# The passage from the output projection into the feed-forward products, in another order

## The chip, the cores and the metric

The kernel runs on one core of one Trainium2 chip. The metric is the device time of one execution in microseconds (us), taken as the median of several runs.

## What is computed

Two layers of a hybrid encoder run over 576 tokens: 512 of a prompt and 64 of a sample (d_model 1024, feed-forward width 2816, all in float32). The part that matters here is the end of a layer, cut from the reference:

```python
merged = concat([rms_norm(o_att), rms_norm(o_gm)], -1)   # 1024 wide
x = x + merged @ p['w_o']
h2 = rms_norm(x, p['g_ffn'])
x = x + (silu(h2 @ p['w_gate']) * (h2 @ p['w_up'])) @ p['w_down']
```

## The kernel before

All activations lie transposed, features on the 128 partitions and 576 tokens along the row: `xT` holds x in 8 tiles of 128 features. Float32 products are made from split operands: a high part (`hs_hi`, `w_hi`, `t_hi`: a copy in the fp32r format) and a low part (`hs_lo`, `w_lo`, `t_lo`: the value less its high part); each product is three matmuls, hi x hi, hi x lo and lo x hi. ScalarE makes high parts, VectorE the low parts of activations, GpSimd the low parts of weights.

**The engines' order.** Nothing is scheduled by a tool. Each engine has its own program, written out by hand and run in order, with waits on semaphores between them. `Ring` and `Slots` count, while the program is planned, which value of `full` (TensorE's finished products) and of the other semaphores a reader has to wait for, and which PSUM bank is free.

**The output projection.** `w_o` is done in eight output tiles (`out_tile`), in the order `W_O_ORDER`: tiles 0, 4, 1, 5, 2, 6, 3, 7. A tile is 48 matmuls of 288 columns (8 tiles of features, 3 matmuls, 2 halves of the tokens). VectorE adds each tile to x (`add`, L1665), ScalarE squares it (`square`, L949) and GpSimd adds the squares up (`sum_squares`, L770) in `sumsq`.

**The feed-forward products.** Gate and up matrices are taken in blocks of 256 columns, and each block is multiplied by Strassen's scheme: 7 products of quarter size (12 matmuls each) instead of 8. Products P1 and P2 use parts of x (`hs_hi`, `hs_lo`), P6, P5, P4, P7 and P3 use sums. On the side of x these are four sums t1 to t4 of halves of x per pair of feature tiles (`x_sum(k)`, L1676 to L1684, k from 0 to 3; ScalarE scales an operand first in `x_scale`), split by ScalarE (`t_high`, L1175) and VectorE (`x_low`, L1690). On the side of the weights VectorE adds quarters (`sum_in`, `w_sum`, L1703), ScalarE copies (`high_in`) and GpSimd subtracts (`low_piece`, L861): five pieces per matrix, two of them without a sum. `sum_in(j, up_in, gate_in, 1)` for j from 0 to 3 are the sums of the first up block, `sum_in(j, n0, up_in, 2)` those of the loop's first gate block. `L["g0"]` is the first gate block, `L["u0"]` the first up block; the other ten pairs of blocks, with the down projection, run in a loop.

**The passage.** `first_block` is written for the stretch in which x is not finished. TensorE begins with the parts of P6, P5 and P4 for k = 0, 1, 2 (27 matmuls), then P1 (its parts k need `hs_lo` of tiles 0 to 3, columns 0 to 287), then the last quarters of P6, P5, P4 (k = 3), P7, the squares' sum by token (`sums_by_token`, L1945, ten tiny matmuls), P2 (tiles 4 to 7) and P3. ScalarE copies P1 out (`first_product`, L1204). VectorE's `evict` forms u2 (L1728, from P6) and u3 (L1731, from P7), and c22, c21, c11, c12 from the rest; P7 waits for u2, P3 for c22. `evict` calls a function handed over in `between` after a named step.

**The root.** The normalization factor is 1/sqrt of the mean square: `r_asked` reads the token sums out of PSUM, GpSimd takes the root (`root`, L761), `r_taken` copies it (L1364), TensorE spreads it over the columns (`r_along_columns`, L2259) and VectorE copies it to `rb` and multiplies the gate block by it (L1821), before its own loop preparations and the up block's `evict`.

VectorE's program in the passage, as it stands before (L1797 on):

```python
add(3)
for j in range(4):
    sum_in(j, up_in, gate_in, 1)
add(7)
x_sum(3)
for k in range(4):
    low_part(2 * l + 1, k, g_ffn, half)
x_low(3)
low_part(2 * l + 1, 4, g_ffn)
```

GpSimd waits for the last `x_low` before it adds squares 6 and 7 (L883).

## Time and profile before

| | |
|---|---|
| median of 3 runs | 1406.43 us |
| lowest and highest | 1401.91 and 1406.65 us |
| the profiled execution | 1408.31 us |
| its span in the profile | 1406.5 us |
| TensorE busy | 1349.6 us, 96% of the span |
| VectorE, ScalarE, GpSimd busy | 912.5, 600.2, 855.4 us |
| mean granted TensorE clock | 0.983 of full speed |

In the profile L numbers are lines of the kernel, PE is TensorE's matmuls, PEld its weight loads, DVE VectorE, ACT ScalarE, POOL GpSimd. A matmul of 288 columns is listed with some 0.29 us, but the next one starts 0.13 us after it: starts tell the pace. Behind "<-" in brackets stands what ended the idle time. All times in a timeline are from the start of the span.

### The profile page before, as it was taken

The page shows a single profiled execution, that of the slowest core. Times are in us where ns is not written, and L with a number is a line of the kernel's source. Part 1 is how long each engine was busy: PE and PEld are TensorE (multiplying, and loading weights), DVE is VectorE, ACT ScalarE, POOL GpSimd, SP SyncE. Part 2 cuts the span into 40 slices and gives each one's busy share as a digit, 9 for nine tenths or more (in the row PEclk, how much of TensorE's full clock was granted, in tenths as well). Part 3 has the DMA queues.
Part 4 walks back from the last instruction along what each step waited for, and adds up shares of the span by engine and source line. Part 5 has one row for each costly group of instructions (what it writes and reads, how often), then busy time and mean ns, then how long its engine had stood idle before and what let it go on. Part 6 is the DMA issues. An engine that isn't in the chain of part 4 may idle for free.

```text
span 1406.5 us, 25387 instructions
## 1 busy us (share of the span) xinstructions
PE 1349.6 (96%) x9462; PEld 1245.9 (89%) x9462; DVE 912.5 (65%) x1490; ACT 600.2 (43%) x956; POOL 855.4 (61%) x452
## 2 busy tenths in 40 slices
PE   8999989989999999999999989989899999999998
PEld 7885667989999999999988656779899999999997
DVE  3456567586676767676736465756876666666664
ACT  6237476353333333333432455763433333333331
POOL 2445247377777777777654534455687777777771
PEclk9999999999999999999999999999999999999999
DMA  7200022122333222222412000221122223223221
GB/s 231 83 16 15 1 60 61 31 61 85 92 91 92 89 90 90 90 89 89 130 61 68 11 5 1 61 61 54 41 87 91 89 90 90 91 89 91 91 85 68
DMA packets 138593, 102.35 MB, mean 73 GB/s; under 512 B 8988, under 2 KB 125152, under 8 KB 138528
## 3 DMA queue, kind: packets, MB, share of 16 engines
q1 hardware_dynamic: 135864, 100.46, 23.6%
q10 hardware_dynamic: 2664, 1.02, 0.3%
q8 instruction: 42, 0.69, 0.2%
q14 instruction: 23, 0.19, 0.0%
HBM read 98.10 MB, written 3.36 MB: 72 GB/s over the span
## 4 chain that ended last, share of the span: by engine, by line
PE 84%; DVE 8%; ACT 2%; issue 2%; POOL 2%; DMA 1%; ACTq 0%; SPq 0%; DVEq 0%
PE ps L2234 34%; PE ps L1932 9%; PE ps L1933 9%; PE ps L1936 9%; PE ps L1878 4%; PE ps L1915 3%; PE ps L1917 3%; PE ps L1916 3%; PE ps L2175 2%; PE ps L2155 2%; POOL rs L761 2%; PE ps L2039 2%; PE ps L2045 1%; PE ps L2132 1%; DVE hs_lo L1330 1%
## 5 line engine op out<-in xcount | busy, mean ns | idle before, releaser
L761 POOL TENSOR_TENSOR rs<-ms,mhalf 128x8 f32<-128x8 f32 (+5 forms) x66 | 139.7, 2120 | 196.8 <-DVE ms L1468 78.9
L861 POOL TENSOR_TENSOR w_lo<-raw,w_hi 128x1024 fp32r<-128x1024 f32 x132 | 229.8, 1768 | 42.4 <-ACT w_hi L1281 39.7
L1703 DVE TENSOR_REDUCE raw<-raw 128x512 f32<-128x1024 f32 x184 | 230.5, 1254 | 0.5
L861 POOL TENSOR_TENSOR w_lo_a<-raw,w_hi_a 128x512 fp32r<-128x512 f32 x88 | 179.6, 2053 | 69.9 <-ACT w_hi_a L1281 69.9
L1932 PE MATMUL ps<-act_hi,w_hi 128*128 128x288 f32 x704 | 196.6, 294 | 3.5 <-issue 3.5
L1933 PE MATMUL ps<-act_lo,w_hi 128*128 128x288 f32 x704 | 196.9, 295 | 0.0
L1665 DVE TENSOR_TENSOR xT<-ps,xT 128x576 f32<-128x576 f32 x192 | 142.2, 750 | 46.9 <-PE ps L1936 46.8
L2234 PE MATMUL ps<-t_hi,w_hi 128*128 128x288 f32 x528 | 157.8, 299 | 7.4 <-DVE side L1728 6.2
L2234 PE MATMUL ps<-t_lo,w_hi 128*128 128x288 f32 x528 | 157.3, 298 | 0.0
L2234 PE MATMUL ps<-t_hi,w_lo 128*128 128x288 f32 x528 | 157.0, 297 | 0.0
L754 POOL TENSOR_TENSOR w_lo<-raw,w_hi 128x2048 fp32r<-128x2048 f32 (+1 forms) x21 | 93.4, 4452 | 97.8 <-ACT w_hi L929 97.8
L1936 PE MATMUL ps<-act_hi,w_lo 128*128 128x288 f32 x704 | 150.9, 296 | 0.0
L1281 ACT ACTIVATE w_hi<-raw 128x512 fp32r<-128x512 f32 (+1 forms) x120 | 88.8, 770 | 121.7 <-DVE raw L1703 121.7
L1932 PEld LDWEIGHTS ps<-act_hi,w_hi 128*128 128x128 f32 x704 | 132.9, 189 | 3.9 <-issue 3.9
L1933 PEld LDWEIGHTS ps<-act_lo,w_hi 128*128 128x128 f32 x704 | 133.0, 189 | 0.0
L909 POOL TENSOR_TENSOR w_lo<-raw,w_hi 128x2048 fp32r<-128x2048 f32 x20 | 92.5, 4625 | 66.4 <-ACT w_hi L1295 66.4
L1936 PEld LDWEIGHTS ps<-act_hi,w_lo 128*128 128x128 f32 x704 | 113.3, 189 | 0.0
L2234 PEld LDWEIGHTS ps<-t_hi,w_hi 128*128 128x128 f32 x528 | 99.9, 189 | 8.7 <-issue 7.0
L2234 PE MATMUL ps<-hs_hi,w_hi_a 128*128 128x288 f32 x352 | 104.0, 296 | 3.7 <-DVE hs_lo L1330 3.7
L2234 PE MATMUL ps<-hs_hi,w_lo_a 128*128 128x288 f32 x352 | 103.5, 294 | 0.0
L2234 PE MATMUL ps<-hs_lo,w_hi_a 128*128 128x288 f32 x352 | 103.3, 293 | 0.0
L2234 PEld LDWEIGHTS ps<-t_hi,w_lo 128*128 128x128 f32 x528 | 100.8, 191 | 0.0
(245 smaller groups left out, 3473.1 us busy)
## 6 DMA issues: line engine op xcount, KB each, us to landing
raw<-in_w_gate SPq DMA_DIRECT2D x88, 256.0 KB, 3.7
raw<-in_w_up SPq DMA_DIRECT2D x88, 256.0 KB, 3.6
raw<-in_w_down SPq DMA_DIRECT2D x20, 1024.0 KB, 4.9
raw<-in_w_in SPq DMA_DIRECT2D x9, 1024.0 KB, 5.2
raw<-in_w_o SPq DMA_DIRECT2D x16, 512.0 KB, 5.5
x_tm<-in_x_prompt SPq DMA_DIRECT2D x4, 512.0 KB, 4.9
raw<-in_w_down SPq DMA_DIRECT2D x8, 256.0 KB, 3.5
out_y_prompt<-x_tm SPq DMA_DIRECT2D x8, 256.0 KB, 2.2
```

Of the source, the lines that this page charges most:

```text
L754: pool.tensor_tensor(w_lo[:, k % 2, 0:size], raw[:, n % 2, 0:size], w_hi[:, k % 2, 0:size].bitcast(F32), ALU.subtract).then_inc(lo_split, 1)
L761: pool.tensor_tensor(rs[:, c:c + n], ms[:, c:c + n], mhalf[:, 0:n], ALU.pow).then_inc(rs_ready, 1)
L861: pool.tensor_tensor(lo[:, k, cols], src, hi[:, k, cols].bitcast(F32), ALU.subtract).then_inc(lo_split, 1)
L909: pool.tensor_tensor(w_lo[:, k % 2, :], raw[:, n % 2, :], w_hi[:, k % 2, :].bitcast(F32), ALU.subtract).then_inc(lo_split, 1)
L1281: act.activation(hi[:, k, cols], src, ACT.Copy).then_inc(hi_split, 1)
L1665: return dve.tensor_tensor(x, ps[:, u.bank:u.bank + 2, 0:HALF], x, ALU.add)
L1703: dve.tensor_reduce(raw[:, 2, j * Q:(j + 1) * Q], added(a, b), AX.X, ALU.add).then_inc(sums_added, 1)
L1878: return pe.transpose(dst, src, ident[0:n, 0:n])
L1932: pe.matmul(bank(u, cols=HALF), hi, x_hi[:, k, cols], start=first, stop=False)
L1933: pe.matmul(bank(u, cols=HALF), hi, x_lo[:, k, cols], start=False, stop=False)
L1936: ins = pe.matmul(bank(u, cols=HALF), lo, x_hi[:, k, cols], start=False, stop=last)
L2234: ins = pe.matmul(bank(u, cols=HALF), a_w[:, k_w, w], x_k(k), start=start, stop=False, skip_group_check=True)
```

## The change

- The last output tile takes its feature tiles in the order 0 to 7, and TensorE signals when its first half is done (`wo_half`). ScalarE makes the high parts of tiles 0 to 3 (which write over what that half has read) after that signal, and those of tiles 4, 5, 6 directly after the whole tile.
- On VectorE the low parts of tiles 0 to 3 come before the last addition to x; two of the four weight sums of the first up block come behind the whole `evict` of the gate block.
- The last split of sums (k = 3) is cut in two halves on ScalarE and VectorE, with a count of their own; TensorE's last quarters wait for the half they use.
- Low part 7 comes behind u3. GpSimd adds squares 6 and 7 only when all low parts are made. Odd squares go to `hid[:, 1]` instead of `gate[:, 1]`.
- The squares' sum by token stands behind P3 on TensorE instead of before P2, and the spreading of the root behind P6 of the up block instead of behind P1.

```diff
-        L["wo"] = {m: [ring.add("wo_added", with_last=h > 0) for h in range(2)] for m in W_O_ORDER}
+        L["wo"] = {}
+        for no, m in enumerate(W_O_ORDER):
+            if no == KT - 1:
+                L["wo_half"] = ring.mark()
+            L["wo"][m] = [ring.add("wo_added", with_last=h > 0) for h in range(2)]
...
-        L["g0"] = block(L["ffn_in"][0], FIRST_PRODUCTS, {"P7": sums})
+        L["g0"] = block(L["ffn_in"][0], FIRST_PRODUCTS, {"P3": sums})
...
-        L["u0"] = block(L["ffn_in"][1], between={"P1": columns})
+        L["u0"] = block(L["ffn_in"][1], between={"P6": columns})
...
+        def squares_of(m, no):
+
+            if m % 2 == 0 and no % 2:
+                return hid[:, 1, :]
+            return gate[:, no % 2, :]
...
-                pool.wait_ge(t_lo_done, KT // 2 * (l + 1))
+                pool.wait_ge(hs_lo_done, (2 * l + 2) * KT)
                 sum_squares(2 * l, [6, 7])
                 low_piece(up_in, 2)
                 root(l, "r2", NT)
...
-                filled(act, L["wo"][W_O_ORDER[-1]][1])
+                filled(act, L["wo_half"])
                 for k in range(4):
                     high_part(k, g_ffn, half)
-                t_high(3)
+                filled(act, L["wo"][W_O_ORDER[-1]][1])
+                for k in range(4, 7):
+                    high_part(k, g_ffn)
+                t_high(3, 0, 2)
+                t_high(3, 2, 4)
+                first_product(L["g0"], L["g0"].out["u2"] - 1)
                 square_output(7)
-                high_part(4, g_ffn)
+                high_part(7, g_ffn)
                 high_in(up_in, 2, slots.last[L["w_o"][3]], SUMS * l + 4)
-                high_part(5, g_ffn)
-                high_part(6, g_ffn)
-                first_product(L["g0"], L["g0"].out["u2"] - 1)
-                high_part(7, g_ffn)
...
-                for j in range(4):
+                for j in range(2):
                     sum_in(j, up_in, gate_in, 1)
+                for k in range(4):
+                    low_part(2 * l + 1, k, g_ffn, half)
                 add(7)
                 x_sum(3)
-                for k in range(4):
-                    low_part(2 * l + 1, k, g_ffn, half)
-                x_low(3)
+                x_low(3, 0, 2)
+                x_low(3, 2, 4, 1)
                 low_part(2 * l + 1, 4, g_ffn)
...
-                def more_low_parts():
-                    for k in range(5, KT):
+                def low_parts(first, last):
+                    for k in range(first, last):
                         low_part(2 * l + 1, k, g_ffn)
-                    dve.wait_ge(summed, (2 * l + 1) * KT)
 
                 evict(L["g0"], first_p1 + 1, gate, None, (0, 0, 0), None,
-                      {"u2": more_low_parts, "c22": lambda: r_asked(L["ss2"]),
-                       "c11": lambda: r_taken(l, "r2", 2 * l + 2)})
+                      {"u2": lambda: low_parts(5, 7), "u3": lambda: low_parts(7, KT),
+                       "c21": lambda: dve.wait_ge(summed, (2 * l + 1) * KT - 1)})
+                r_asked(L["ss2"])
+                for j in range(2, 4):
+                    sum_in(j, up_in, gate_in, 1)
+                r_taken(l, "r2", 2 * l + 2)
...
-                    out_tile(no)
+                    if no < KT - 1:
+                        out_tile(no)
+                        continue
+                    out_tile(no, range(KT // 2)).then_inc(full, 1)
+                    out_tile(no, range(KT // 2, KT))
...
                     made("u2")
                     product(b.b, w_sum(2), k_w, x_sum(2), False)
-                    pe.wait_ge(summed, (2 * l + 1) * KT)
-                    sums_by_token(L["ss2"], [sumsq])
                     pe.wait_ge(p1_out, copied)
                     product(b.a, a_part(1), k_w, x_part(1, 0), False, ready=lambda k: part_due(k + KT // 2))
                     pe.wait_ge(lo_split, split + 5)
                     made("c22")
                     product(b.c, w_sum(3), k_w, x_part(1, 1), False)
+                    pe.wait_ge(summed, (2 * l + 1) * KT)
+                    sums_by_token(L["ss2"], [sumsq])
...
                     product(b.a, a_part(0), k_w, x_part(0, 0), True)
-                    between()
                     pe.wait_ge(lo_split, split + 3)
                     free_in_turn(b.b)
                     product(b.b, w_sum(1), k_w, x_sum(1), True)
+                    between()
```

VectorE at the start of the passage, from the split of the sums k = 2 on, before the change (`xT<-ps,xT` is an addition to x, `raw<-raw` a weight sum, `hs_lo` a low part, `side` u2):

```order
L1690 TENSOR_TENSOR t_lo<-x_sums,t_hi 128x4x288
L1665 TENSOR_TENSOR xT<-ps,xT 128x576
L1703 TENSOR_REDUCE raw<-raw 128x512 x4
L1665 TENSOR_TENSOR xT<-ps,xT 128x576
L1676 SCALAR_TENSOR_TENSOR x_sums<-xT,gT,x_sums 128x288
L1679 SCALAR_TENSOR_TENSOR x_sums<-xT,gT,x_sums 128x288
L1682 SCALAR_TENSOR_TENSOR x_sums<-xT,gT,x_sums 128x288
L1684 SCALAR_TENSOR_TENSOR x_sums<-xT,gT,x_sums 128x288
L1330 SCALAR_TENSOR_TENSOR hs_lo<-xT,gT,hs_hi 128x288 x4
L1690 TENSOR_TENSOR t_lo<-x_sums,t_hi 128x4x288
L1330 SCALAR_TENSOR_TENSOR hs_lo<-xT,gT,hs_hi 128x576
L1728 TENSOR_TENSOR side<-ps,side 128x288
```

The same place after the change:

```order
L1702 TENSOR_TENSOR t_lo<-x_sums,t_hi 128x4x288
L1677 TENSOR_TENSOR xT<-ps,xT 128x576
L1715 TENSOR_REDUCE raw<-raw 128x512 x2
L1342 SCALAR_TENSOR_TENSOR hs_lo<-xT,gT,hs_hi 128x288 x4
L1677 TENSOR_TENSOR xT<-ps,xT 128x576
L1688 SCALAR_TENSOR_TENSOR x_sums<-xT,gT,x_sums 128x288
L1691 SCALAR_TENSOR_TENSOR x_sums<-xT,gT,x_sums 128x288
L1694 SCALAR_TENSOR_TENSOR x_sums<-xT,gT,x_sums 128x288
L1696 SCALAR_TENSOR_TENSOR x_sums<-xT,gT,x_sums 128x288
L1702 TENSOR_TENSOR t_lo<-x_sums,t_hi 128x2x288 x2
L1342 SCALAR_TENSOR_TENSOR hs_lo<-xT,gT,hs_hi 128x576
L1740 TENSOR_TENSOR side<-ps,side 128x288
```

The four low parts now stand ahead of the addition of tile 7 and of the sums of x; two weight sums have left.

VectorE from u3 of the gate block to u2 of the up block, before the change (`ms` and `r_tok` belong to the root, `rb` to the spread factor):

```order
L1731 TENSOR_TENSOR side<-ps,side 128x288
L1734 TENSOR_TENSOR gate<-side,ps 128x288
L1356 TENSOR_SCALAR ms<-ps 128x5
L1359 COPY ms<-ms 128x5
L1737 TENSOR_TENSOR gate<-side,ps 128x288
L1746 COPY gate<-ps 128x288
L1364 COPY r_tok<-rs 128x5
L1749 TENSOR_TENSOR gate<-ps,side 128x288
L1816 COPY rb<-ps 128x512
L1818 COPY rb<-ps 128x64
L1821 TENSOR_TENSOR gate<-gate,rb 128x576 x2
L1703 TENSOR_REDUCE raw<-raw 128x512 x2
```

The same place after the change, without the first two rows' like (u3 and low part 7 stand ahead of it):

```order
L1747 TENSOR_TENSOR gate<-side,ps 128x288
L1750 TENSOR_TENSOR gate<-side,ps 128x288
L1759 COPY gate<-ps 128x288
L1762 TENSOR_TENSOR gate<-ps,side 128x288
L1368 TENSOR_SCALAR ms<-ps 128x5
L1371 COPY ms<-ms 128x5
L1715 TENSOR_REDUCE raw<-raw 128x512 x2
L1376 COPY r_tok<-rs 128x5
L1833 COPY rb<-ps 128x512
L1835 COPY rb<-ps 128x64
L1838 TENSOR_TENSOR gate<-gate,rb 128x576 x2
L1715 TENSOR_REDUCE raw<-raw 128x512 x2
```

The root is asked for behind the whole `evict`, and the two weight sums stand between the question and the copy of its answer.

## Rows read from the trace of the kernel before

**Rows 1.** The page: busy us by engine, and the chain by engine.
```profile
PE 1349.6 (96%) x9462; PEld 1245.9 (89%) x9462; DVE 912.5 (65%) x1490; ACT 600.2 (43%) x956; POOL 855.4 (61%) x452
...
PE 84%; DVE 8%; ACT 2%; issue 2%; POOL 2%; DMA 1%; ACTq 0%; SPq 0%; DVEq 0%
```

**Rows 2.** Stretches: length, busy us (instructions) of each engine, PEclk, DMA share, GB/s.
```profile
304.04:338.39 34.35, 28.80 (x190) 27.74 (x189) 27.99 (x39) 16.03 (x24) 23.79 (x15) 0.90 0.20 61
996.94:1031.30 34.36, 28.82 (x191) 27.76 (x189) 28.00 (x39) 16.03 (x24) 23.81 (x15) 0.90 0.20 60
400.00:600.00 200.00, 200.00 (x1512) 200.00 (x1511) 136.42 (x194) 73.30 (x99) 149.63 (x75) 1.00 0.30 90
```

**Rows 3.** Timeline of TensorE in the first passage: start, us, line, operation [idle before].
```profile
309.62 0.37 PE L2234 MATMUL ps<-hs_hi,w_hi_a 128*128 128x288 f32 x1 [1.84 <-DVE hs_lo L1330]
...
312.09 0.40 PE L2234 MATMUL ps<-t_hi,w_hi 128*128 128x288 f32 x1 [0.61 <-DVE t_lo L1690]
...
314.70 0.50 PE L2234 MATMUL ps<-t_hi,w_hi 128*128 128x288 f32 x1 [1.15 <-DVE side L1728]
...
317.64 1.44 PE L1945 MATMUL ps<-ones,sumsq 128*128 128x1 f32 x10
...
330.43 0.37 PE L2234 MATMUL ps<-t_hi,w_hi 128*128 128x288 f32 x1 [1.93 <-DVE side L1728]
```

**Rows 4.** Stretches of one microsecond, columns as in rows 2.
```profile
316.00:317.00 1.00, 1.00 (x6) 1.00 (x6) 1.00 (x2) 0.00 (x0) 1.00 (x1) 0.50 0.00 0
333.00:334.00 1.00, 1.00 (x6) 1.00 (x6) 0.98 (x2) 0.00 (x0) 1.00 (x2) 0.50 0.00 0
```

**Rows 5.** Timeline of ScalarE: the last scaling and the four high parts.
```profile
301.05 0.52 ACT L1187 ACTIVATE x_sums<-xT,gT 128x288 f32<-128x288 f32 x1
304.24 1.82 ACT L943 ACTIVATE hs_hi<-xT,gT 128x288 fp32r<-128x288 f32 x4 [2.67 <-PE ps L1936]
```

**Rows 6.** Timeline of GpSimd: squares' sums, weight pieces, the root.
```profile
302.12 1.46 POOL L770 TENSOR_TENSOR sumsq<-sumsq,gate 128x576 f32<-128x576 f32 x1
303.50 1.33 POOL L861 TENSOR_TENSOR w_lo_a<-raw,w_hi_a 128x512 fp32r<-128x512 f32 x1
304.77 2.42 POOL L861 TENSOR_TENSOR w_lo_a<-raw,w_hi_a 128x1024 fp32r<-128x1024 f32 x1
...
312.11 3.49 POOL L770 TENSOR_TENSOR sumsq<-sumsq,gate 128x576 f32<-128x576 f32 x2 [4.92 <-DVE t_lo L1690]
...
315.56 2.88 POOL L861 TENSOR_TENSOR w_lo<-raw,w_hi 128x1024 fp32r<-128x1024 f32 x1
...
320.99 1.18 POOL L761 TENSOR_TENSOR rs<-ms,mhalf 128x5 f32<-128x5 f32 x1 [2.56 <-DVE ms L1359]
...
333.93 2.38 POOL L861 TENSOR_TENSOR w_lo<-raw,w_hi 128x1024 fp32r<-128x1024 f32 x1
```

**Rows 7.** Timeline of VectorE in the first passage.
```profile
305.42 0.73 DVE L1665 TENSOR_TENSOR xT<-ps,xT 128x576 f32<-128x576 f32 x1
306.19 1.31 DVE L1676 SCALAR_TENSOR_TENSOR x_sums<-xT,gT,x_sums 128x288 f32<-128x288 f32 x1
...
308.96 1.80 DVE L1330 SCALAR_TENSOR_TENSOR hs_lo<-xT,gT,hs_hi 128x288 fp32r<-128x288 f32 x4
...
310.68 1.35 DVE L1690 TENSOR_TENSOR t_lo<-x_sums,t_hi 128x1152 fp32r<-128x1152 f32 x1
...
314.47 1.75 DVE L1330 SCALAR_TENSOR_TENSOR hs_lo<-xT,gT,hs_hi 128x576 fp32r<-128x576 f32 x1
...
316.14 3.64 DVE L1330 SCALAR_TENSOR_TENSOR hs_lo<-xT,gT,hs_hi 128x576 fp32r<-128x576 f32 x2
...
322.20 1.25 DVE L1364 COPY r_tok<-rs 128x5 f32<-128x5 f32 x1 [0.45 <-POOL rs L761]
...
327.39 2.53 DVE L1703 TENSOR_REDUCE raw<-raw 128x512 f32<-128x1024 f32 x2
...
329.83 0.45 DVE L1728 TENSOR_TENSOR side<-ps,side 128x288 f32<-128x288 f32 x1
```

More of the change, by code:

```diff
@@ L241 @@
 WARM = 24
+T_PARTS = KT // 2 + 1
 SMALL, EARLY_GAINS, LATE_GAINS = 8, 3, 8
@@ L1170, in _, with t_high @@
                     act.activation(hs_hi[:, k, 0:SEQ], bank(u), ACT.Copy, scale=gT[:, g:g + 1]).then_inc(m_hi, 1)
-                def t_high(k):
-                    act.wait_ge(x_summed, 4 * (KT // 2 * l + k + 1))
-                    act.activation(t_hi[:, :, k, :], x_sums[:, k % 2, :, :], ACT.Copy).then_inc(t_hi_done, 1)
+                def t_high(k, c0=0, c1=4):
+                    act.wait_ge(x_summed, 4 * (KT // 2 * l + k) + c1)
+                    act.activation(t_hi[:, c0:c1, k, :], x_sums[:, k % 2, c0:c1, :], ACT.Copy).then_inc(t_hi_done, 1)
                 def square_output(no):
@@ L1184, in x_scale @@
                     if k >= 2:
-                        act.wait_ge(t_lo_done, KT // 2 * l + k - 1)
+                        act.wait_ge(t_lo_done, T_PARTS * l + k - 1)
                     g = G_FFN + KT * l + k
@@ L1685, in x_sum, with x_low @@
                                              ).then_inc(x_summed, 1)
-                def x_low(k):
-                    dve.wait_ge(t_hi_done, KT // 2 * l + k + 1)
-                    dve.tensor_tensor(t_lo[:, :, k, :], x_sums[:, k % 2, :, :], t_hi[:, :, k, :].bitcast(F32), ALU.subtract
-                                      ).then_inc(t_lo_done, 1)
+                def x_low(k, c0=0, c1=4, part=0):
+                    dve.wait_ge(t_hi_done, T_PARTS * l + k + part + 1)
+                    dve.tensor_tensor(t_lo[:, c0:c1, k, :], x_sums[:, k % 2, c0:c1, :], t_hi[:, c0:c1, k, :].bitcast(F32),
+                                      ALU.subtract).then_inc(t_lo_done, 1)
                 def w_sum(j, n, landed, lower, base):
@@ L1731, in evict @@
                     dve.tensor_tensor(u3, p_b, p1, ALU.subtract).then_inc(S["ffn_out"], 1)
+                    follow("u3")
                     made("u3")
@@ L1938, in by_feature @@
                             ins.then_inc(full, 1)
+                return ins
             def sums_by_token(u, tiles):
@@ L2181, in out_tile @@
                 def out_tile(no, ks=None):
-                    by_feature(L["wo"][W_O_ORDER[no]], slots.raw[L["w_o"][no // 2]] % 2, no % 2 * P, COLS, KT, hs_hi, hs_lo,
-                               order=MERGED[1:], ks=ks, ready=None if no else lambda k: emptied(pe, L["mt"][k]))
+                    order = MERGED[1:] if no < KT - 1 else list(range(KT))
+                    return by_feature(L["wo"][W_O_ORDER[no]], slots.raw[L["w_o"][no // 2]] % 2, no % 2 * P, COLS, KT, hs_hi, hs_lo,
+                                      order=order, ks=ks, ready=None if no else lambda k: emptied(pe, L["mt"][k]))
                 pe.wait_ge(gm_normed, NT * (l + 1))
@@ L2268, in made, with sums_due @@
                         pe.wait_ge(S["ffn_out"], b.out[name])
-                    def sums_due(k):
-                        pe.wait_ge(t_lo_done, KT // 2 * l + k + 1)
+                    def sums_due(k, part=0):
+                        pe.wait_ge(t_lo_done, T_PARTS * l + k + part + 1)
                     def part_due(k):
@@ L2282, in first_block @@
                     product(b.a, a_part(0), k_w, x_part(0, 0), True, ready=part_due)
-                    sums_due(3)
-                    for u, w, x in early:
+                    for (u, w, x), part in zip(early, (0, 0, 1)):
+                        sums_due(3, part)
                         product(u, w, k_w, x, False, range(3, 4))
```

4 lines of the change are left out of this document (2 added, 2 removed).

## The prediction

> **What bounds the kernel now.** I read the page's busy row and its chain first. TensorE is busy for 96% of the span and has 84% of the chain that ended last [rows 1], so a change that adds no matmul pays only where TensorE stands still. The table of stretches tells where that is [rows 2]. Between 400 and 600 us, inside the feed-forward loop, 1512 matmuls fill 200.00 us: 0.132 us each, at full clock, without a gap. In the passage, from the first matmul on sums of x at 304.04 to the first of the loop at 338.39, 168 products' matmuls should take 168 x 0.132 = 22.2 us and the stretch has 34.35 us. The second layer's passage has 34.36 us. So the passage loses 12.1 us per layer, 24 us in all, 1.7% of the kernel; nothing else is touched.
>
> The timeline of TensorE in that stretch shows the loss [rows 3]: four gaps, of 1.84, 0.61, 1.15 and 1.93 us by the rows. The first ends when the low parts of x are there, the second with the low parts of the sums, the other two with u2 of the first and of the second block. A chain of ten tiny matmuls (the squares' sum by token, 1.3 us to the next product) stands between P7 and P2 of the first block, and ten more between two products of the second. The rest is clock: the windows at 316 and 333 us hold 6 matmuls per us, granted 0.50 (1.2 GHz), against 7.6 at full clock [rows 4]; each time some 12 matmuls cost 0.24 instead of 0.13 us, 1.3 us.
>
> **Where VectorE and GpSimd meet.** They hold each other up. Four low parts of 288 columns take 1.80 us, 0.45 each, at 308.96 when GpSimd stands idle; one of 576 columns takes 1.75 us at 314.47, ending 0.6 us after GpSimd's sums (312.11 for 3.49) have ended at 315.60; the next two take 3.64 us at 316.14, while GpSimd's split (315.56 for 2.88) ends at 318.44 [rows 6, 7]. The split in turn took 2.88 instead of 2.42 us: it waited for the low part. The weight sums (tensor_reduce, one operand) and the additions out of PSUM are not held up. So: an instruction of VectorE with two operands in SBUF starts when GpSimd's running instruction has ended, and GpSimd's next one waits for it; they alternate.
>
> The Trainium skill, page SBUF — State Buffer, in its section on the two separate sides, speaks against this change: VectorE's instructions with two SBUF inputs and GpSimd's share one exclusive lock, held for a whole instruction. By bare durations the low parts would be 1.8 us of work wherever they are put, and the sum would come out near the first rival below; by the lock it comes out as below. The rows above show the lock.
>
> **The change, step by step** (times as in the trace of before; first layer).
>
> 1. *The half signal.* The last output tile's 48 matmuls end at 304.04, so its first half ends 24 x 0.132 = 3.2 us sooner, 300.9. ScalarE is busy to about 301.5 with the scaling at 301.05, then makes the four high parts at 301.5 to 303.3 instead of 304.24 to 306.06 [rows 5]: 2.7 us sooner.
>
> 2. *VectorE.* The addition of tile 3 and two weight sums end at 302.9 (two sums take 2.53 [rows 7]). Now the four low parts are due, before the last addition. GpSimd runs its sum from 302.12 to 303.58, a piece of 512 (303.50, some 1.3) and one of 1024 (2.42) [rows 6]. Alternating: low part 0 ends at 303.9, GpSimd's 512 at 305.2, low part 1 at 305.6, GpSimd's 1024 at 308.0, low parts 2 and 3 at 308.8. What would be 1.8 us takes 5.9. The addition of tile 7 follows, 308.8 instead of 305.42. The two other weight sums (2.5 us) have left, so the four steps of the sums of x run free, each about 0.53: 309.5 to 311.6 against 306.19 to 309.0 before (the low parts start at 308.96). The cut in halves saves 0.5 us: the first half's low part is ready at 311.9, the second at 312.7, against 312.03 for the whole [rows 7].
>
> 3. *TensorE, first block.* P1 starts right behind the early ones, 307.6 instead of 309.62; its last quarter waits for low part 3 and ends at 309.2. Then the gap moves: 2.7 us until 311.9. u2 comes behind low part 4 and is ready at about 313.9, and P7 starts at 314.1 instead of 314.70: gain 0.6. The squares' chain is gone from here; low parts 5 and 6 run free, GpSimd waiting. Low part 7 now waits for u3, so for P7's end (about 316.2): ready at 317.4. P2 ends at 317.9, P3 at 319.5, where before the chain of ten sat at 317.64 and P3 ended at 322.4: 2.9 us gained so far.
>
> 4. *The squares' sum comes later.* GpSimd adds the last two squares only after low part 7: 317.4 to 320.2 (1.4 each; before they began at 312.11). TensorE waits 0.9 us, runs its ten, and P1 of the second block starts at 321.5: 0.9 of the 2.9 us is left. GpSimd then has the third up piece (2.4) before the root (1.18): the root ends at 323.8, where before it ended at 322.17 [rows 6]. VectorE is at the two delayed weight sums from 322.0 to 324.6, and its copy of the roots, which needs the lock (1.25 us for 5 columns at 322.20 [rows 7]), waits for GpSimd's next piece: done at 325.3 instead of 323.45, 1.85 late. The spreading over columns on TensorE, which stood 6.4 us ahead of u2 together with the two rb copies, two multiplications and two more weight sums (323.45 to 329.83 [rows 7]), is 5.9 us now, since c12 has gone ahead: u2 at 331.2, 1.4 late. P6 of the up block no longer waits behind the spreading, but its P7 waits for u2: gap from 328.0 to 331.8, where it was 328.3 to 330.43.
>
> 5. *The squares in another buffer, the counter T_PARTS, two instructions more on VectorE and ScalarE:* nothing, since ScalarE stands idle from 306 to 309 and the added halves are in step 2. The load of w_down waits for the last up piece and is issued some 2 us later than now; its weights are used 10 us after it landed, so it hides there.
>
> Sum: the loop begins 1.4 us later per layer, if both half-clock stretches stay as they are. Two layers: +2.8 us. The profiled execution took 1408.31 us (span 1406.5), so 1411.1; it stands 1.9 above the median of the three runs, 1406.43, and against that median the forecast is **1409.2 us**. Bounds per layer: the alternation costs 4.1 us in step 2 at most and nothing at least; the half-clock stretches may become none (-2.6) or three (+1.3).
>
> **Rivals.**
> - *The low parts slip through* (the other side). If GpSimd's pieces do not hold the low parts, they end at 304.8 and the addition of tile 7 at 305.5; the first step of the sums of x still waits for GpSimd until 307.2, as now, the halves are ready at 309.1 and 309.9, P7 starts at 311.3, 2.8 us sooner than in my sum, and all behind it follows: the loop begins 1.4 us sooner than before, 2.8 us in all, 1403.6. For: only low parts of 576 columns were seen held. Against: the first step of the sums, also 288 columns, took 1.31 us at 306.19 and ended 0.3 us after GpSimd's 1024 piece [rows 6, 7]. The sign turns once the low parts lose less than 2.7 us to GpSimd instead of 4.1. Chance 0.2.
> - *The clock goes another way.* Gaps of 2.7 and 3.8 us replace smaller ones, four in number as before; which matmuls run at 1.2 GHz depends on where the idle lies. One stretch fewer in each layer: 2.6 us off, 1406.6. Chance 0.15. One more in each, or the slow stretch falling on a full product: 2.6 to 4 us on, 1412 to 1413. Chance 0.12.
> - *The tail starves the loop.* GpSimd's first pieces for the loop end 1.4 to 2 us later. The third now ends at 336.3 (333.93 for 2.38 [rows 6]) and is wanted by the loop's second product, 12 x 0.132 = 1.6 us after 338.39, at 340.0, so 1.5 us or more remain. If they do not, each layer loses another 2 us: 1413. Chance 0.05.
>
> The forecast itself has 0.48.
>
> **How the numbers follow.** About 0.5%, 7 us, is what a measurement of this kernel can tell from no change. Faster than 1399.4 needs the first rival and a lost clock stretch: 0.12. Slower than 1413.5 needs the forecast and an added stretch in both layers, or a mis-sized step 4: 0.16. The rest, 0.72, is within. The range takes in the first rival, less one lost clock stretch (1403.6 - 2.6 = 1401.0), and the slower clock at 1413.5.
>
> **What would show it.** Right: in the profile after, P1 of the first block starts at once behind the early products; the low parts of 288 columns spread over some 5 us between GpSimd's pieces; a gap of over 2 us sits in front of the last quarter of the early products; the gap in front of the second block's u2 is over 3 us. Wrong: four low parts within 2 us, a passage shorter than 33 us, or u2 of the second block ahead of 25.8 us after the passage's start.

## The result, and the profile after

| | before | after |
|---|---|---|
| median of 12 runs each | 1407.84 us | 1413.3 us |
| lowest and highest | 1401.91, 1411.86 | 1409.52, 1418.38 |
| the profiled execution | 1408.31 | 1413.44 |
| its span | 1406.5 | 1411.6 |
| mean granted TensorE clock | 0.983 | 0.981 |

The ratio is 1.0039, with a 95% interval of 1.0023 to 1.0056: the kernel is 5.5 us slower. That is 0.4%, less than the 0.5% that the prediction took as what a measurement can tell, but the interval is clear of 1. The forecast was 2.8 us slower, 1409.2 us, in a range to 1413.5.

The stretches of the trace after, with the columns of [rows 2]: the two passages, the last four products of the first passage, and a piece of the loop.

```profile
307.36:344.89 37.53, 30.15 (x190) 29.04 (x189) 28.06 (x39) 14.63 (x21) 24.15 (x15) 0.86 0.18 56
1000.05:1037.86 37.81, 29.89 (x190) 28.76 (x189) 28.06 (x39) 14.63 (x21) 24.14 (x15) 0.86 0.18 55
335.67:344.89 9.22, 9.22 (x48) 9.22 (x49) 5.10 (x7) 2.60 (x4) 8.89 (x5) 0.66 0.01 3
403.00:603.00 200.00, 200.00 (x1512) 200.00 (x1511) 136.40 (x194) 74.06 (x99) 147.09 (x74) 1.00 0.31 94
```

The loop is what it was, 1512 matmuls in 200 us. The passages are 3.2 and 3.5 us longer than the 34.35 and 34.36 us of [rows 2], 6.6 us together. This profiled execution is only 5.1 us longer than that of before, since the rest of it comes out 1.5 us shorter. No instruction was changed there, but half-clock stretches outside the passages fall at other places (the granted clock is 0.50 from 823.4 to 830.2 us before, and from 133.7 to 140.5 us after); that these make up the 1.5 us was not worked out.

The timeline of TensorE after, first passage; the gaps answer to [rows 3].

```profile
315.16 0.40 PE L2257 MATMUL ps<-t_hi,w_hi 128*128 128x288 f32 x1 [2.49 <-DVE t_lo L1702]
...
317.19 0.37 PE L2257 MATMUL ps<-t_hi,w_hi 128*128 128x288 f32 x1 [0.53 <-DVE side L1740]
...
323.36 0.83 PE L1963 MATMUL ps<-ones,sumsq 128*128 128x1 f32 x6 [0.78 <-POOL sumsq L781]
...
335.66 0.58 PE L2257 MATMUL ps<-t_hi,w_hi 128*128 128x288 f32 x1 [3.49 <-DVE side L1740]
336.04 0.45 PE L2257 MATMUL ps<-t_lo,w_hi 128*128 128x288 f32 x1
336.28 0.45 PE L2257 MATMUL ps<-t_hi,w_lo 128*128 128x288 f32 x1
```

The 1.84 us gap ahead of P1 is gone. In its place stand 2.49 us ahead of the last early quarters, and in front of the second block's P7 3.49 us instead of 1.93. Behind that gap the starts are 0.24 us apart, at half clock. In the second layer the gap ahead of u2 of the first block is gone, one of 1.07 us stands ahead of the spreading of the root, and P7 has 3.50 us in front of it.

VectorE after, from the low parts on, answering to [rows 7]:

```profile
306.14 5.54 DVE L1342 SCALAR_TENSOR_TENSOR hs_lo<-xT,gT,hs_hi 128x288 fp32r<-128x288 f32 x4
311.60 0.75 DVE L1677 TENSOR_TENSOR xT<-ps,xT 128x576 f32<-128x576 f32 x1
312.38 0.52 DVE L1688 SCALAR_TENSOR_TENSOR x_sums<-xT,gT,x_sums 128x288 f32<-128x288 f32 x1
...
325.56 2.59 DVE L1715 TENSOR_REDUCE raw<-raw 128x512 f32<-128x1024 f32 x2
328.06 0.85 DVE L1376 COPY r_tok<-rs 128x5 f32<-128x5 f32 x1
330.45 0.69 DVE L1833 COPY rb<-ps 128x512 f32<-128x512 f32 x1 [1.54 <-PE ps L2282]
...
331.31 1.43 DVE L1838 TENSOR_TENSOR gate<-gate,rb 128x576 f32<-128x576 f32 x2
332.66 2.50 DVE L1715 TENSOR_REDUCE raw<-raw 128x512 f32<-128x1024 f32 x2
335.08 0.44 DVE L1740 TENSOR_TENSOR side<-ps,side 128x288 f32<-128x288 f32 x1
```

Four low parts of 288 columns took 1.80 us in [rows 7]; here they take 5.54. The last row is u2 of the second block, 27.7 us after the passage's start (335.08 - 307.36), where it was 25.8 (329.83 - 304.04). GpSimd shows why the root is late: the last two squares begin at 320.33, 13.0 us into the passage, where in [rows 6] they began at 312.11, 8.1 us in.

```profile
305.46 1.42 POOL L781 TENSOR_TENSOR sumsq<-sumsq,hid 128x576 f32<-128x576 f32 x1
306.85 4.08 POOL L872 TENSOR_TENSOR w_lo_a<-raw,w_hi_a 128x512 fp32r<-128x512 f32 x2
320.33 1.42 POOL L781 TENSOR_TENSOR sumsq<-sumsq,gate 128x576 f32<-128x576 f32 x1 [9.39 <-DVE hs_lo L1342]
321.89 1.42 POOL L781 TENSOR_TENSOR sumsq<-sumsq,hid 128x576 f32<-128x576 f32 x1
323.26 2.35 POOL L872 TENSOR_TENSOR w_lo<-raw,w_hi 128x1024 fp32r<-128x1024 f32 x1
325.73 1.18 POOL L772 TENSOR_TENSOR rs<-ms,mhalf 128x5 f32<-128x5 f32 x1
```

### The profile page after: what moved, and what is told of

It is laid out like the page before. It is cut to its first block, busy times and chain, and to the rows that moved or that the text cites. A ratio compares the mean times of both kernels' runs of the same rounds, so it can differ in the third digit from the quotient of the medians.

```text
span 1411.6 us, 25389 instructions
## 1 busy us (share of the span) xinstructions
PE 1350.9 (96%) x9462; PEld 1247.5 (88%) x9462; DVE 913.9 (65%) x1492; ACT 600.5 (43%) x958; POOL 853.4 (60%) x452
## 4 chain that ended last, share of the span: by engine, by line
PE 84%; DVE 9%; ACT 2%; POOL 2%; issue 2%; DMA 1%; ACTq 0%; SPq 0%; DVEq 0%; POOLq 0%
PE ps L2257 34%; PE ps L1949 9%; PE ps L1953 9%; PE ps L1950 9%; PE ps L1895 4%; PE ps L1932 3%; PE ps L1933 3%; PE ps L1934 3%; PE ps L2193 2%; PE ps L2173 2%; DVE hs_lo L1342 2%; POOL rs L772 2%; PE ps L2057 2%; PE ps L2063 1%; PE ps L2150 1%
```

## The experiments

In all of them times are given from the start of the passage (the first matmul on sums of x), and "P7" alone is that of the second block. "Half clock costs" is what the matmuls that start while the granted clock is 0.50 lose against 0.132 us each, summed over the passage (worked out from the starts in the timelines). Executions of one kernel lie 6 to 17 us apart, with the granted clock over the whole of them, so where there is a single one the passage in its trace is the measurement, and not the time. Each ratio is to executions of the kernel before on the same chip; their medians were 1407.23 to 1409.14 us, and 1404.36 us for the last row.

| kernel | P7 of block 1 | P7 | loop begins | half clock costs | gap ahead of P7 | ratio to before |
|---|---|---|---|---|---|---|
| before, layers 1 / 2 | 10.7 / 10.7 | 26.4 / 26.4 | 34.4 / 34.4 | 2.5 / 2.5 | 1.9 | 1 |
| after | 9.8 / 10.2 | 28.3 / 28.7 | 37.5 / 37.8 | 4.1 / 3.7 | 3.5 | 1.0039 [1.0023, 1.0056] |
| low parts back | 9.4 / 9.3 | 27.8 / 27.8 | 35.8 / 35.8 | 2.9 / 2.8 | 3.5 | one execution |
| GpSimd waits | 9.6 / 8.6 | 28.7 / 27.1 | 36.5 / 35.0 | 4.0 / 2.8 | 3.5 | one execution |
| spreading back | 10.1 / 9.3 | 28.6 / 27.6 | 35.0 / 34.0 | 1.1 / 1.0 | 1.9 | one execution |
| sums back | 10.6 / 10.3 | 29.4 / 29.0 | 38.3 / 37.9 | 4.8 / 3.7 | 3.5 | one execution |
| squares back | 9.3 / 10.2 | 27.8 / 28.3 | 36.8 / 36.1 | 3.4 / 2.3 | 3.6 | one execution |
| front alone | 9.7 / 10.6 | 26.5 / 27.1 | 34.5 / 35.0 | 2.6 / 3.5 | 1.9 | 0.9989 [0.9961, 1.0016] |
| tail alone | 10.7 / 10.6 | 30.1 / 30.5 | 38.1 / 38.5 | 3.0 / 4.1 | 3.5 | 1.0063 [1.0038, 1.0087] |
| after, P4 ahead | 10.1 / 9.3 | 28.6 / 27.8 | 33.5 / 32.7 | 1.2 / 1.5 | 1.9 | 1.0001 [0.9971, 1.0031] |
| after, u2 first | 9.3 / 10.5 | 25.1 / 26.6 | 31.6 / 33.0 | none / 1.1 | 1.1 | 1.0 [0.997, 1.003] |
| before, u2 first | 10.7 / 10.7 | 24.3 / 24.3 | 30.7 / 30.7 | 1.1 / 1.1 | none | 0.9967 [0.9943, 0.999] |
| front, u2 first | 10.3 / 9.7 | 25.1 / 24.4 | 31.4 / 30.8 | 1.0 / 1.1 | none | 0.9979 [0.9958, 0.9999] |
| before, P4 ahead | 10.6 / 10.7 | 26.4 / 26.4 | 31.3 / 31.3 | none / 1.1 | 0.4 | 1.0003 [0.9976, 1.0031] |

### Is it the low parts, and does GpSimd hold them?

Two kernels on the changed one. First the low parts at their old place:

```diff
-                for k in range(4):
-                    low_part(2 * l + 1, k, g_ffn, half)
                 add(7)
                 x_sum(3)
+                for k in range(4):
+                    low_part(2 * l + 1, k, g_ffn, half)
```

> The changed kernel with one part undone: on VectorE the addition of tile 7 and the sums of x stand ahead of the four low parts again. All numbers from the passage's first matmul on sums of x. Lock theory (low parts of 288 columns wait for GpSimd's pieces): the four low parts take 1.8 us in one go instead of 5.4, the last quarter of the early products starts at 7.6 instead of 7.8, P7 at 9.5 instead of 9.8, and the loop begins within 0.4 us of the changed kernel's 37.5, because the tail (root, two late weight sums, u2 behind two loop sums) is as it was. Rival (the low parts' place is what made the kernel slower): the loop begins at 35 or sooner, the time falls by 5 us or more.

Second, the low parts ahead as in the change, but GpSimd's pieces wait for them:

```diff
                 sum_squares(2 * l, [5])
+                pool.wait_ge(hs_lo_done, (2 * l + 1) * KT + 4)
                 low_piece(up_in, 0)
```

> The changed kernel with one wait added: GpSimd starts the first two pieces of the up matrix only when low parts 0 to 3 are made. Lock theory: the four low parts take 1.8 us in one go at the place where the change puts them, and the addition of tile 7 moves from 4.2 us to about 1.1 us after the passage's start; the sums of x then meet GpSimd's two pieces and lose most of it again, P7 starts at 9.3 instead of 9.8 and the loop begins 0.3 to 0.5 us sooner. Rival (GpSimd doesn't hold VectorE up, the low parts wait for something else, such as ScalarE's high parts): the low parts keep their spread over 5 us and nothing moves.

VectorE in the first (an addition, two steps of the sums of x, then the low parts):

```profile
311.55 0.53 DVE L1688 SCALAR_TENSOR_TENSOR x_sums<-xT,gT,x_sums 128x288 f32<-128x288 f32 x1
312.11 2.54 DVE L1691 SCALAR_TENSOR_TENSOR x_sums<-xT,gT,x_sums 128x288 f32<-128x288 f32 x1
...
315.55 1.80 DVE L1342 SCALAR_TENSOR_TENSOR hs_lo<-xT,gT,hs_hi 128x288 fp32r<-128x288 f32 x4
```

and in the second:

```profile
303.98 2.36 DVE L1343 SCALAR_TENSOR_TENSOR hs_lo<-xT,gT,hs_hi 128x288 fp32r<-128x288 f32 x4
306.26 0.75 DVE L1678 TENSOR_TENSOR xT<-ps,xT 128x576 f32<-128x576 f32 x1
307.04 0.99 DVE L1689 SCALAR_TENSOR_TENSOR x_sums<-xT,gT,x_sums 128x288 f32<-128x288 f32 x1
308.06 2.54 DVE L1692 SCALAR_TENSOR_TENSOR x_sums<-xT,gT,x_sums 128x288 f32<-128x288 f32 x1
```

The same low parts take 5.54, 1.80 and 2.36 us, by what GpSimd runs beside them: its two pieces, nothing, and the end of its addition of squares (303.30 to 304.73), which holds the first low part until 305.05. What is next in VectorE's queue then meets the pieces instead: one step of 0.52 us takes 2.54, the length of GpSimd's piece of 1024. So the mutual holding up is real, and in each of these three orders some of it was paid while GpSimd's two pieces lay in these 4 us. Moving it is worth 0.5 to 0.8 us at block 1's P7 with the low parts back, 0.2 and 1.5 us with GpSimd waiting (at 9.6 and 8.6, where 9.3 was expected). The gap of 3.5 us ahead of the second block's P7 stays in both, and P7 stands 18.5 us behind P7 of block 1 in both layers with the low parts back, as after the change (15.7 before): so the loss of P7 lies behind block 1. The loop, however, begins at 35.8 with the low parts back, which neither expectation had (37.1 to 37.9, or 35 and sooner), and at 36.5 and 35.0 with GpSimd waiting, where some 37 was expected. The clock is most of that: from P7 to the loop TensorE takes 8.0 us with the low parts back and 7.8 and 7.9 with GpSimd waiting, instead of 9.2. The times were 1414.95 and 1413.14 us, not shorter than after the change.

### Front alone, tail alone

The front is the half signal, ScalarE's order, the low parts and the halves; the tail is the squares' sum with low part 7 behind u3, the spreading and the two weight sums. The front alone undoes these lines of the change:

```diff
-        L["g0"] = block(L["ffn_in"][0], FIRST_PRODUCTS, {"P3": sums})
+        L["g0"] = block(L["ffn_in"][0], FIRST_PRODUCTS, {"P7": sums})
-        L["u0"] = block(L["ffn_in"][1], between={"P6": columns})
+        L["u0"] = block(L["ffn_in"][1], between={"P1": columns})
-                pool.wait_ge(hs_lo_done, (2 * l + 2) * KT)
+                pool.wait_ge(t_lo_done, T_PARTS * (l + 1))
                 sum_squares(2 * l, [6, 7])
-                for j in range(2):
+                for j in range(4):
                     sum_in(j, up_in, gate_in, 1)
```

with VectorE's `between` functions and TensorE's two calls as they were; the tail alone makes just these, reversed, in the kernel before, with the squares' other buffer.

> The front of the change alone: half signal, ScalarE's new order, low parts ahead of the last addition, halves of the last split; the squares' sum, the spreading of the roots and all four weight sums at their old places. Theory A (the tail made the kernel slower, the front is worth next to nothing): the passage from first matmul on sums of x to the loop is 34 to 35 us (before 34.35, changed 37.5 and 37.8), P7 of the second block at 26.4 +-0.5, the time within 1.5 us of before (ratio 1.000 +-0.001). Rival B (the spread low parts of the front carry a part of the loss): the passage stays at 36 us or more, ratio 1.002 or more.

> The tail of the change alone, on the kernel before: the squares' sum behind the first block's last product and in another buffer, the spreading of the roots behind P6, two weight sums behind the first block; no half signal, old order of the low parts, the last split whole. Theory A (the tail carries the loss): P7 of the first block at 10.0 to 10.7, P1 of the second at 17.5 to 18.2, P7 of the second at 28 to 28.8 (before 26.4), the loop at 36.5 to 38 (before 34.35), some +2 to +3.5 us per layer, ratio 1.003 to 1.005. Rival B (the loss comes from the front, or from front and tail together): the loop at 35.5 or sooner, ratio under 1.002.

```profile
302.38:336.83 34.45, 28.88 (x190) 27.80 (x189) 29.33 (x39) 14.53 (x21) 23.59 (x15) 0.90 0.18 56
990.79:1025.83 35.04, 29.90 (x190) 28.91 (x189) 29.91 (x40) 14.53 (x21) 24.18 (x15) 0.85 0.19 59
```

are the two passages of the front alone, and

```profile
303.36:341.45 38.09, 29.18 (x191) 27.86 (x189) 27.37 (x39) 16.14 (x24) 22.80 (x15) 0.91 0.18 55
999.91:1038.36 38.45, 30.60 (x190) 29.32 (x189) 27.33 (x39) 16.14 (x24) 22.79 (x15) 0.87 0.17 54
```

those of the tail alone. The tail costs 3.7 and 4.1 us per layer and more time than the whole change (1.0063); the front costs 0.1 and 0.7 us in the trace and nothing in the time. Joined with the tail the front gives back 0.6 us per layer. The first theory holds: the tail is what made the kernel slower. It was expected to bring P7 to 28 to 28.8, the loop to 36.5 to 38 and the ratio to 1.003 to 1.005; all three came out beyond (30.1 and 30.5, 38.1 and 38.5, 1.0063). And its loss lies in the lateness of P7 alone. From P7 to the loop, in these rows of the stretches, the kernel before and the tail alone take the same time, although the gap in front is 1.93 us in the one and 3.50 in the other:

```profile
330.43:338.39 7.96, 7.96 (x48) 7.96 (x49) 5.04 (x7) 2.62 (x4) 7.96 (x5) 0.79 0.00 1
333.48:341.45 7.97, 7.97 (x49) 7.97 (x49) 5.04 (x7) 2.60 (x4) 7.97 (x5) 0.79 0.01 3
```

Why the front gains nothing in the end can be read too: it brings P7 of block 1 forward by 0.9 and 0.1 us, but GpSimd begins squares 6 and 7 0.5 and 1.0 us later (8.6 and 9.1 us into the passage, 8.1 before), and the roots are copied at 19.5 and 20.1 instead of 19.4.

### Which part of the tail?

Each undone by itself in the changed kernel. The spreading behind P1 again:

```diff
-        L["u0"] = block(L["ffn_in"][1], between={"P6": columns})
+        L["u0"] = block(L["ffn_in"][1], between={"P1": columns})
...
                     product(b.a, a_part(0), k_w, x_part(0, 0), True)
+                    between()
...
                     product(b.b, w_sum(1), k_w, x_sum(1), True)
-                    between()
```

> The changed kernel with one thing undone: in the second block TensorE spreads the roots over the columns right behind P1, as before, and no longer behind P6. Theory A (u2 of the second block is late because VectorE's queue ahead of it starts late, and about 1 us of that is TensorE finishing P6 before it spreads): the first copy of rb starts about 22.1 us after the start of the passage instead of 23.1, u2 comes 1 us sooner, the second block's P7 starts at 27.3 instead of 28.3 and the loop at 36.5 instead of 37.5; the gap ahead of P7 shrinks from 3.5 to some 1.5 us and a new one of 2.5 to 3 us stands ahead of P6. Rival B (the place of the spreading is hidden behind the late roots): P7 stays at 28.3, the loop at 37.5. Either way 2 us of the whole at most, so the passage in the trace decides.

The two weight sums ahead again (`range(2)` to `range(4)`, the later loop gone):

> The changed kernel with one thing undone: the two weight sums of the up weights that came later stand again right behind the first two, ahead of the four low parts. Theory A (they are not what makes u2 late, since VectorE does them while it waits for the root anyway): the low parts come up to 2.5 us later but run in fewer turns with GpSimd, P7 of the first block starts at 10.4 instead of 9.8, the copy of the roots ends at 21.0 to 21.5 (now 21.55), P7 of the second block starts at 27.7 to 28.3, the loop at 37 to 37.5. Rival B (the two sums in front of the copy of the roots hold it up by their 2.5 us): the copy ends by 19.5 to 20, P7 at 26.3, the loop at 35.5.

The squares' sum early again, its matmuls between P7 and P2, `r_asked` behind c22 and `r_taken` behind c11, low part 7 with the others behind u2:

```diff
-                pool.wait_ge(hs_lo_done, (2 * l + 2) * KT)
+                pool.wait_ge(t_lo_done, T_PARTS * (l + 1))
...
-                r_asked(L["ss2"])
                 for j in range(2, 4):
                     sum_in(j, up_in, gate_in, 1)
-                r_taken(l, "r2", 2 * l + 2)
```

> The changed kernel with one thing undone: the squares' sum and its ten matmuls at their old place between P7 and P2 of the first block, VectorE asking and taking the roots as before; the spreading stays behind P6, the two weight sums stay behind the first block. Theory A (the late squares' sum is the largest single part of the tail's loss): the copy of the roots ends at 18 to 19.5 us instead of 21.55, u2 of the second block at 25.8 to 27, its P7 at 26.5 to 27.7 and the loop at 34.5 to 35.7, the gap ahead of P7 below 3 us. Rival B (the roots come sooner but u2 stays behind VectorE's queue of sums, copies and products): P7 at 28 or later, the loop at 37 or more.

No single part brings P7 back to 26.4: it stands at 28.6 and 27.6, 29.4 and 29.0, 27.8 and 28.3. In time they were 1405.72, 1413.57 and 1413.93. With the squares back VectorE shows how one lateness hides another:

```profile
324.90 0.17 DVE L1376 COPY r_tok<-rs 128x5 f32<-128x5 f32 x1 [0.44 <-POOL rs L772]
...
325.91 2.63 DVE L1715 TENSOR_REDUCE raw<-raw 128x512 f32<-128x1024 f32 x2
329.42 0.69 DVE L1832 COPY rb<-ps 128x512 f32<-128x512 f32 x1 [0.88 <-PE ps L2281]
```

The roots are copied at 325.07, 18.0 us into the passage (start 307.09) and 3.6 us sooner than after the change (21.55). But now the two late weight sums and the spreading behind P6 stand between them and u2, and rb is copied at 22.3 instead of 23.1, only 0.8 us sooner. P7 (27.8 and 28.3) came out between the two expectations in the first layer and as the second had it in the other, the loop (36.8 and 36.1) between them. With the sums back the low parts start later, P1 of the second block starts at 19.1 and 18.8 instead of 17.1 and 17.7, and the squares that all wait for come later (ten matmuls at 18.0 and 17.6 instead of 16.0 and 16.6); the roots are copied at 22.8 and 22.5, and both expectations had the roots and P7 too early. With the spreading back P7 does not move by itself either: it stands at 28.6 and 27.6, but 18.5 and 18.3 us behind P7 of block 1, against 18.5 after the change. That is as the second theory said, yet the loop begins at 35.0 and 34.0, sooner than either had it. TensorE there:

```profile
328.03 1.38 PE L2282 MATMUL ps<-ident,r_tok 128*128 128x128 f32 x10 [2.63 <-DVE r_tok L1376]
...
334.53 0.37 PE L2257 MATMUL ps<-t_hi,w_hi 128*128 128x288 f32 x1 [1.93 <-DVE side L1740]
```

The idle time is cut in two pieces, 2.63 and 1.93 us, in place of one of 3.49 (in the second layer 1.49 and 1.93). The four products behind it run at full clock, in this row of the stretches:

```profile
334.52:340.98 6.46, 6.45 (x48) 6.46 (x49) 5.54 (x6) 1.94 (x3) 6.46 (x4) 1.00 0.00 1
```

6.46 us instead of 9.22 for the same 48 matmuls: 2.8 and 2.7 us in the two layers from the clock alone.

### The gap itself: P4 ahead of P7

P4 needs no u2. On TensorE alone, in the changed kernel:

```diff
+                    free_in_turn(b.d)
+                    product(b.d, a_part(2), k_w, x_sum(3), True)
                     pe.wait_ge(lo_split, split + 4)
                     made("u2")
                     product(b.b, w_sum(2), k_w, x_sum(2), False)
-                    free_in_turn(b.d)
-                    product(b.d, a_part(2), k_w, x_sum(3), True)
```

(for the first up block alone, with `FIRST_PRODUCTS` as the order in its plan).

> The changed kernel with one move on TensorE: in the second block P4, which needs no u2, ahead of P7. It changes nothing on VectorE, so u2 stays at 27.7 us after the passage's start and P7 at 28.3; the gap ahead of P7 is 1.9 instead of 3.5 us. Theory A (the gap of 3.5 us as one piece is what brings the half-clock stretch of 6.8 us behind it, some 2.8 us per layer): the loop begins at 33 to 34.5 us (now 37.5 and 37.8), 4 us sooner per layer, ratio to before 0.997 to 1.000. Rival B (the clock falls behind P7 anyway, whatever the gap's length): only the 1.6 us of P4 are won, the loop at 35.9 to 36.2, ratio 1.001 to 1.003.

```profile
300.96:334.44 33.48, 27.14 (x190) 26.00 (x189) 26.94 (x38) 13.95 (x20) 20.13 (x13) 0.95 0.20 62
991.07:1023.74 32.67, 27.39 (x190) 26.27 (x189) 26.40 (x38) 13.96 (x20) 19.63 (x13) 0.95 0.19 60
```

u2 is as late as it was (28.1 and 27.2), P7 starts at 28.6 and 27.8, and the loop begins 4.1 and 5.1 us sooner. The filled gap is 1.6 us of that. The 36 matmuls from P7 to the loop take 4.84 us, at full clock, where P7, P4, P2 and P3 took 9.22:

```profile
329.60:334.44 4.84, 4.84 (x36) 4.84 (x37) 3.94 (x6) 1.92 (x3) 4.84 (x3) 1.00 0.01 2
```

That is 2.8 us from the clock in each layer, what the first theory had; what is left, -0.3 and +0.8 us, is P7 itself, which comes with P7 of block 1. A new gap of 1.11 us opens in the loop's first block, outside the passage. The ratio is 1.0001 instead of 1.0039. It goes the same way, but its interval reaches to 1.0031 and just overlaps that of the change, so by the time alone the second theory (1.001 to 1.003) is not ruled out; the passages rule it out.

The same move in the kernel before:

> The kernel before with one move on TensorE: P4 of the second block ahead of P7, which fills its gap of 1.93 us but for 0.3. Theory A (a gap filled is worth its length, and the half-clock stretch behind it goes too, as in the same move on the changed kernel): P7 of the second block still at 26.4, behind P4, so that the loop begins at 31.4 to 32.7 us instead of 34.35, ratio 0.995 to 0.998. Rival B (the clock falls at the same place for what lies ahead of it): the loop at 32.7 or later, ratio 0.998 or more. The move of u2 on VectorE gave 30.7 us and 0.9967 for the same gap.

The passage is 31.26 and 31.27 us, 3.1 less than before, and here too a new gap of 1.11 us opens behind it in the loop:

```profile
339.40 0.40 PE L2234 MATMUL ps<-t_hi,w_hi 128*128 128x288 f32 x1 [1.11 <-DVE side L1728]
```

That leaves 2.0 us per layer, 4 in all, and a ratio of 0.997 was to be expected. The measured one is 1.0003, with an interval of 0.9976 to 1.0031. The profiled execution took 1400.2 us, others up to 1416.6. So the gain is seen in the one execution that has a trace and not in the median, and whether this move pays stays open.

### u2 first

VectorE does two weight sums for the loop ahead of u2 of the second block, 2.5 us for something that is wanted later. In the changed kernel and in the one before:

```diff
-                for j in range(2):
-                    sum_in(j, n0, up_in, 2)
+                def loop_sums():
+                    for j in range(3):
+                        sum_in(j, n0, up_in, 2)
...
-                      {"u2": lambda: sum_in(2, n0, up_in, 2), "c22": lambda: sum_in(3, n0, up_in, 2), "c21": gate_due})
+                      {"u2": loop_sums, "c22": lambda: sum_in(3, n0, up_in, 2), "c21": gate_due})
```

> The changed kernel with u2 of the up block made ahead of the loop's first two weight sums on VectorE (they follow directly behind it). Queue theory (u2 is late only because of what stands ahead of it on VectorE): P7 of the up block starts 2.5 us sooner, at 25.8 instead of 28.3 us of the passage, the gap in front of it shrinks from 3.5 to about 1 us, with it a stretch of half clock may vanish, and the loop begins 2.5 to 4 us sooner: 5 to 8 us less in all, 1405 to 1408. Rival (GpSimd's piece for P7 or the late root sets it): P7 gains less than 1 us, and the time stays within 2 us of the changed kernel's.

> The kernel before with the same one move as e3_u2_first. Queue theory: P7 of the up block starts 1.9 to 2.4 us sooner, the gap of 1.93 us in front of it closes, the half-clock stretch behind it goes with it (1.3 us), and the loop begins 2 to 3.7 us sooner: 1401 to 1404 against 1407.8, faster by 0.3 to 0.5%. Rival: the pieces of the loop's first block, now made 0.5 us later, hold up the loop's first products, and the time stays the same.

VectorE of the kernel before with this move, to be set beside the last rows of [rows 7]:

```profile
324.82 1.43 DVE L1821 TENSOR_TENSOR gate<-gate,rb 128x576 f32<-128x576 f32 x2
326.17 0.45 DVE L1728 TENSOR_TENSOR side<-ps,side 128x288 f32<-128x288 f32 x1
326.53 3.73 DVE L1703 TENSOR_REDUCE raw<-raw 128x512 f32<-128x1024 f32 x3
```

and its passages and the two new gaps of TensorE in the loop's first block:

```profile
302.79:333.50 30.71, 27.08 (x191) 26.23 (x189) 27.20 (x39) 15.37 (x24) 20.13 (x13) 0.94 0.22 68
995.54:1026.19 30.65, 27.09 (x190) 26.23 (x189) 27.14 (x39) 15.38 (x24) 20.09 (x13) 0.94 0.22 68
```

```profile
335.75 0.40 PE L2235 MATMUL ps<-t_hi,w_hi 128*128 128x288 f32 x1 [0.51 <-POOL w_lo L861]
...
339.99 0.40 PE L2235 MATMUL ps<-t_hi,w_hi 128*128 128x288 f32 x1 [0.77 <-DVE side L1728]
```

The gap ahead of P7 is gone, the passage is 3.6 and 3.7 us shorter, 1.3 us of it come back in the loop. That is 2.4 us per layer, 4.8 in all, and the ratio of 0.9967 [0.9943, 0.999] is 4.6 us: 1403.91 us, where before had 1409.14 on the same chip. **This version beats both kernels**, by 0.3% the kernel before. In the changed kernel the same move takes away what the change had lost, 1408.42 against 1409.14. There P7 starts at 25.1 and 26.6 (25.8 was expected) and the loop begins 5.9 and 4.8 us sooner, more than the 2.5 to 4 expected, since no half-clock stretch follows P7; gaps of 0.8 and 0.8 us in the loop's first block take 1.6 of it back.

Does the front help once u2 is out of the way?

> The front of the change alone, and on VectorE u2 of the second block ahead of the two weight sums for the loop (the move that made the kernel before faster by 0.33%). Theory A (the front is worth next to nothing, since the squares' chain and the roots set the pace behind it): the passage is 30.5 to 31.3 us, like the 30.7 us of the kernel before with the same move, P7 of the second block at 24.2 to 24.8 without a gap, ratio 0.995 to 0.999. Rival B (with u2's own delay gone, the front's 0.5 to 1 us ahead of P7 of the first block comes through): passage 29.7 us or less, ratio under 0.995.

The passages are 31.4 and 30.8 us and the ratio 0.9979 [0.9958, 0.9999]: no better than 0.9967, as the first theory had it (the first passage 0.1 us over its bound). Behind P7 of block 1 stand the squares' chain and the roots, and these came no sooner: the roots are copied at 20.1 and 19.5 us, where the kernel before with the same move has 19.4.

## Why the prediction was right, and where its sizes were not

Direction and range were right, the difference was 2.7 us short. That 1413.3 lies inside a range to 1413.5 is luck in part: the kernel before came out at 1407.84 instead of 1406.43, and the margin left is 0.2 us. The mechanism that was forecast is the one in the trace; one term of the sum was too small. By its steps:

1. *Steps 1 and 2, the half signal and VectorE.* Forecast: low parts spread over 5.9 us, tile 7's addition 4.8 us into the passage. Measured 5.54 and 4.2. The alternation with GpSimd was read rightly out of [rows 6, 7]. The Trainium skill, page SBUF — State Buffer, section on the two separate sides, has the exclusive lock; the trace agrees (1.80 us alone, 5.54 beside GpSimd).
2. *Step 3, TensorE in block 1.* P1 forecast at 3.6, measured 3.58; gap forecast 2.7, measured 2.49; P7 forecast at 10.1, measured 9.8 and 10.2.
3. *Step 4, the late squares.* TensorE's wait forecast 0.9, measured 0.78; P1 of the second block forecast at 17.5, measured 17.1 and 17.7; the copy of the roots done at 21.3, measured 21.55. This was the step that decides, and the tail alone showed it. Its last part was short: u2 1.4 us late by forecast, 1.9 measured, and the second block's P7 at 27.8 by forecast, at 28.3 and 28.7 measured.
4. **The sum, "if both half-clock stretches stay as they are".** This is the term that was mis-sized. The second one did not stay (granted 0.50 from 331.8 to 335.2 us before, from 335.0 to 341.9 after): from P7 to the loop TensorE took 7.96 us before and 9.22 and 9.16 after, 1.2 us more per layer. Together with the 0.5 and 0.9 us of step 4 that is the 3.2 and 3.5 us per layer instead of 1.4. The branch of the second rival, "one more in each", with 1412 to 1413, describes what happened, since one stretch became twice as long. Its 0.12 looks small for a forecast that itself made the longest gap 1.9 us longer. But the longer stretch does not follow from that gap alone: the tail alone and the low parts back have the same 3.5 us and took 8.0 us from P7 to the loop. What decides its length stays open. A reading of [rows 4] was wrong as well: x6 counts every matmul that overlaps the microsecond, and only four and five start in the two shown. The 1.3 us per stretch were worked out from 0.24 us a matmul and do not rest on it; by the starts 12 and 14 matmuls are slow.
5. *The first rival.* Its mechanism fell (the low parts did not slip through), and so did its arithmetic: it let all behind the low parts come 2.8 us sooner once GpSimd no longer holds them. With GpSimd waiting for them they did slip through but for 0.56 us, and the next steps of x met the same pieces; P7 of block 1 came 0.2 and 1.5 us sooner.
6. *What was costed at nothing* (the squares' other buffer, counters, the load of w_down) stayed so. The tail did not starve the loop: TensorE of the changed kernel waits for nothing in the loop.

The passages account for 6.6 us, of which the late u2 is 4.2 and the clock behind it 2.4; the 1.1 us between that and the 5.5 of the medians are less than executions of one kernel differ by.

## What to carry to other kernels

When a wait is moved, follow it to the engine that serves everybody, here VectorE between the roots and u2, and ask what stands in that queue that nobody waits for yet; moving two such sums behind u2 gave 4.6 us, while the front of the reordering alone gave nothing clear of noise (0.9989 [0.9961, 1.0016]) and added nothing to that move (0.9979). Of several reorderings that meet at one instruction, test them all and each alone: undone singly none of the three of the tail brought P7 back, undone together they did (26.5 and 27.1). And the clock is a second price of a gap: here two gaps of 2.63 and 1.93 us, or one partly filled, cost less than one of 3.5, in the passages of one trace each. In the kernel before the filled gap did not show in the median, so the order on the busiest engine is worth a try, and measuring.
